# Low parts of P before the scores of the unit two ahead, on VectorE, in both attention stages

## The chip, the core and the metric

One core of a Trainium2 chip runs the whole program as one launch. The metric is the device time of that launch in microseconds. The program leaves PE (TensorE, matmuls and transposes), DVE (VectorE), ACT (ScalarE), POOL (GpSimd) and SP (the queue that issues most DMAs) to run their own instruction streams in order; they meet only at semaphores.

## The reference, cut to what matters

Two transformer blocks on a sequence of 1024 rows of width 1024. Each holds one attention stage.

```python
# first block: 6 query heads of 64, each block of 128 queries sees 3 blocks of keys
scores = jnp.einsum('bnqkgd,bnskd->bnkgqs', qb, kb).astype(jnp.float32) + bias
m = jnp.maximum(jnp.max(scores, axis=-1, keepdims=True), sink_l)
p = jnp.exp(scores - m)
p = p / (jnp.sum(p, axis=-1, keepdims=True) + jnp.exp(sink_l - m))
out = jnp.einsum('bnkgqs,bnskd->bnqkgd', p.astype(v.dtype), vb)
...
# second block: mixer A, 8 heads, windows of 128 keys behind the query, with a sink;
# mixer B, 8 heads, three dilated causal windows merged by their denominators
out_a = sink_swa_gqa(q_a, k_a, v_a, sinks[i], rel_bias[:, :A_Q_HEADS])
out_b = dilated_mixture(q_b, k_b, v_b, rel_bias[:, A_Q_HEADS:])
```

Around the attention stand the norms, the projections and the feed-forward layers, which the change leaves alone.

## The kernel before

The attention is cut into **units**: unit m is one block of 128 queries of one head, `b = m % 8`, so eight units make a head. A unit has as many blocks of 128 keys as the head's window asks for: two or three in the first stage (`att_bi`, 6 heads, 48 units), one or two in mixer A (the first 64 units of the second stage, `att_ab`), and b + 1, that is one to eight, in mixer B (the last 64 units, where the three dilated patterns are one causal mask with a table of biases). Four units make a **group**; a head has two.

The precise product is made of a high and a low part of each operand. So the softmax numerators P of a unit go through these steps:

- `scores(m)` on PE, L1823: two matmuls into one of two halves of PSUM (m % 2); it waits until the half was read by the scores of unit m-2.
- `score(m)` on DVE, L1946: adds the bias, writes `pr[m % 3]`, and its read-out `ast` of the row extreme counts `at_s`. It needs the scores in PSUM and the transposes of unit m-3 done.
- `exps(m)` on ACT, L1883: exp in place in `pr`, and a read-out of the row sums (`at_exp`).
- `turn_p(m)` on PE, L1833: transposes P into PSUM, in chunks of up to four blocks of keys. Units of up to four blocks have one chunk, larger ones two. Two PSUM banks take turns, so a chunk waits for the low part of the chunk two before it (`at_lo`).
- `high(m)` on ACT, L1893: the high part `ph` of each chunk (`at_hi`).
- `low_(m)` on DVE, L1956: the low part `pl`, PSUM minus `ph` (`at_lo`).
- After four units, `values(g)` on PE, L1848 (it waits for the last `low_` of the group), `denom(g)` on DVE, L1964 and L1966, `spread(g)` on PE, L1857, `spread_out(g)` on ACT, L1906, and `scale(g)` on DVE, L1975. For every second pair of groups ACT and POOL then split the result (L1911, L1999).

All orders are written out by hand. PE in loop m runs `scores(m + 2)`, `turn_p(m)`, and after the fourth unit one more `scores`, then `values` and `spread`. ACT in loop m runs `exps(m + 1)`, at a group's start `spread_out(g - 1)`, then `high(m)`:

```python
                if m + 1 < s.n:
                    exps(m + 1)
                if m % 4 == 0 and g:
                    spread_out(g - 1)
                high(m)
```

SP loads q and the bias table of head h once all scores of head h-2 are done on DVE (`at_s`, L1740, L1745); `scores` of a head's first unit waits for them.

Of the kernel before, what the change touches and what calls it, by code (L numbers as in the profile page):

```python
# [94 lines left out]
def build(nc, t, out, last=6):  # L95

    ctx = ExitStack()
    with ctx:
# [5 lines left out]
        def S(name):  # L104
            if name not in sems:
                sems[name] = ctx.enter_context(nc.semaphore(name))
            return sems[name]
# [1620 lines left out]
        def tab_dve(e):  # L1728
            e.wait_ge(S("oh_ld"), 48)
            e.memset(relb1[BUCKETS:BUCKETS + 1, :], 1.0).then_inc(S("rb"), 1)  # L1730
            e.tensor_copy(relb1[0:BUCKETS, :], relb[:]).then_inc(S("rb"), 1)
# [201 lines left out]
        def att_dve(e, s, a):  # L1933
            n, g_ = s.h0 * TT, s.h0 * 2
            e.wait_ge(S("sk_ld"), 32)

            def score(m):
                d, b, k0, k1, _ = s.units[m]
                w, r, j0 = (k1 - k0) * P, m % 8, (k0 - b) * P + d.off
                if m >= 3:  # L1940
                    e.wait_ge(S("at_tr"), s.unit_end(m - 3))
                if b == 0:
                    e.wait_ge(S(f"at_q_{s.name}{m // TT % 2}"), 48 * (m // TT // 2 + 1))
                e.wait_ge(S("at_qk"), n + m + 1)
                low = 3e30 if d.sink is None else nsk[:, d.sink:d.sink + 1]
                e.tensor_tensor_reduce(out=a.pr[m % 3][:, 0:w], in0=PSr[:, m % 2 * s.qs:m % 2 * s.qs + w],  # L1946
                                       in1=a.tab[m // TT % 2][:, j0:j0 + w], scale=-0.125, scalar=low, op0=ALU.add,
                                       op1=ALU.min, accum_out=ast[:, NM, r:r + 1]).then_inc(S("at_s"), 1)

            def low_(m):  # L1950
                _, b, _, _, chunks = s.units[m]
                _, kb0, _ = s.group(m // 4)
                for q, c0, c1 in chunks:
                    e.wait_ge(S("at_hi"), s.ch0 + q + 1)
                    o = (slice(None), slice(c0 - kb0, c1 - kb0), slice(b % 4 * P, (b % 4 + 1) * P))
                    e.tensor_tensor(a.pl[o], PS[:, 4 + q % 2, 0:(c1 - c0) * P].rearrange("p (k n) -> p k n", n=P),  # L1956
                                    a.ph[o].bitcast(F32), ALU.subtract).then_inc(S("at_lo"), 1)

            def denom(g):
                c = slice(4 * (g % 2), 4 * (g % 2) + 4)  # L1960
                e.wait_ge(S("at_exp"), n + 4 * g + 4)
                if s.units[4 * g][0].sink is not None:
                    e.wait_ge(S("at_es"), g_ + g + 1)
                    e.tensor_tensor(ast[:, DEN, c], ast[:, DEN, c], ast[:, ES, c], ALU.add).then_inc(S("at_dn"), 1)  # L1964
                    e.wait_ge(S("at_dn"), g_ + g + 1)
                e.reciprocal(ast[:, RD, c], ast[:, DEN, c]).then_inc(S("at_rd"), 1)  # L1966

            def scale(g):
                d = s.units[4 * g][0]
                e.wait_ge(S("at_pv"), g_ + g + 1)  # L1970
                e.wait_ge(S("at_rc"), g_ + g + 1)
                if g % 4 < 2 and g >= 8:
                    e.wait_ge(S("at_yl"), s.h0 + (g // 4 - 2) * 2 + g % 2 + 1)
                r = slice(d.row, d.row + HD)
                e.tensor_tensor(a.t[g // 4 % 2][d.half * HD:(d.half + 1) * HD, g % 2, :], PS[r, 6, :], a.rr[g % 2][r, :], ALU.mult)\  # L1975
                 .then_inc(S("at_nrm"), 1)

            score(0)
            score(1)
            if s is att_bi:  # L1980
                tab_dve(e)
            for m in range(s.n):
                if m + 2 < s.n:
                    score(m + 2)
                if m % 4 == 0 and m:
                    scale(m // 4 - 1)
                low_(m)
                if m % 4 == 3:
                    denom(m // 4)
            scale(s.n // 4 - 1)  # L1990
# [71 lines left out]
        with nc.Block() as block:  # L2062
# [85 lines left out]
            @block.vector  # L2148
            def _(e):
                prep_dve(e)  # L2150
                norm_out_dve(e, 0, 0)
                norm_out_dve(e, 0, 1)
                chain_dve(e)
                late_dve(e, 2)
                z_dve(e, 0)
                fft_dve(e)
                ssm_dve(e)
                att_dve(e, att_bi, mem_bi)
                out_dve(e, 0)
                for f, p in ((0, 1), (1, 2)):  # L2160
                    if last > p:
                        up_dve(e, f)
                        down_dve(e, p)
                if last > 3:
                    z_dve(e, 1)
                    att_dve(e, att_ab, mem_ab)
                    out_dve(e, 3)
                if last > 4:
                    up_dve(e, 2)
                    down_dve(e, 4)  # L2170
                if last > 5:
                    ple_dve(e)
# [53 lines left out]
```

## Time and profile before

| what | value |
|---|---|
| median of 3 runs | 3932.35 us (3929.28 to 3938.76) |
| the profiled execution | 3929.27 us, its span 3927.5 us |
| PE busy | 3391.6 us, 86% |
| DVE busy | 1193.1 us, 30% |
| ACT busy | 790.4 us, 20% |
| first attention stage | about 672 to 819 us of the span |
| second attention stage | about 2605 to 2919 us: mixer A to about 2717, mixer B after it |

The busy shares are those of the whole span. Outside the two stages PE is busy for nine tenths or more of most slices; within them no engine is, so the share of one engine tells little, and the order of steps and the waits between engines are what to read. A timeline row gives the start in us, the duration in us, engine, line, operation, tiles and, in brackets, how long the engine sat idle before and what released it.

### The profile page before, as it was taken

The numbers are of one execution on the slowest core, as the hardware profiler recorded it, in microseconds if no ns is written. First come the engines' busy times: TensorE is split into PE (matmuls) and PEld (weight loads), VectorE is DVE, ScalarE is ACT, GpSimd is POOL, SyncE is SP. The second block draws the span as 40 slices with busy tenths as digits, with TensorE's granted clock in tenths as the row PEclk, the third lists the DMA queues.
The fourth block names the chain that finished last, engine by engine and source line by source line (L and its number), as shares of the span: only waits on it lengthen the run. The fifth ranks groups of instructions, "written<-read, shape, count | busy, mean of one in ns | idle before, by whom it ended". The sixth has DMA issues, their size and how long they took to land.

```text
span 3927.5 us, 41626 instructions
## 1 busy us (share of the span) xinstructions
PE 3391.6 (86%) x15935; PEld 2811.4 (72%) x15935; DVE 1193.1 (30%) x1793; ACT 790.4 (20%) x1395; POOL 1553.2 (40%) x1271
## 2 busy tenths in 40 slices
PE   6773335589999999999999999987778999999977
PEld 4663324477888878888888888876667788888866
DVE  4754664425232322110001123135534100001323
ACT  3020003423111112110000122035533100001222
POOL 3137662044333346622323664210015223236743
PEclk8886666889999999999999999999999999999999
DMA  4551001552111124311112243444433111122432
GB/s 174 149 183 36 7 7 42 87 152 75 43 54 43 54 95 140 102 54 54 43 53 77 96 142 122 143 134 110 108 101 108 49 54 43 53 74 98 151 107 95
DMA packets 261327, 344.92 MB, mean 88 GB/s; under 512 B 24710, under 2 KB 203185, under 8 KB 261202
## 3 DMA queue, kind: packets, MB, share of 16 engines
q1 hardware_dynamic: 217784, 258.76, 21.8%
q10 hardware_dynamic: 43066, 84.01, 6.8%
q8 instruction: 84, 1.38, 0.1%
q0 software_dynamic: 352, 0.44, 0.0%
q14 instruction: 41, 0.34, 0.0%
HBM read 287.21 MB, written 55.95 MB: 87 GB/s over the span
## 4 chain that ended last, share of the span: by engine, by line
PE 75%; DVE 11%; ACT 5%; issue 3%; DMA 3%; POOL 2%; SPq 1%; ACTq 0%; DVEq 0%; POOLq 0%
PE PS L810 68%; PE PS L1848 3%; DMA tab_bi<-bias 1%; DVE ot L1591 1%; PE PS L746 1%; DVE pl_ab L1956 1%; DVE pt L679 1%; PE PS L1543 1%; DVE oo L1592 1%; ACT ph_ab L1893 1%; ACT act L701 1%; DVE t L1607 1%; PE PS L1833 1%; ACT pr_ab L1883 1%; ACT act L653 1%
## 5 line engine op out<-in xcount | busy, mean ns | idle before, releaser
L250 POOL TENSOR_TENSOR w_lo<-w_raw,w_hi 128x512 fp32r<-128x512 f32 x724 | 972.2, 1374 | 155.1 <-ACT w_hi L1302 130.4
L246 POOL CAST w_hi<-w_raw 128x2048 fp32r<-128x2048 f32 x173 | 335.6, 1940 | 1596.2 <-DMA w_raw<-ffn_w_gu 606.8
L810 PE MATMUL PS<-h_hi,w_hi 128*128 128x512 f32 x2482 | 803.2, 395 | 14.3 <-DVE h_lo L804 11.0
L810 PE MATMUL PS<-h_lo,w_hi 128*128 128x512 f32 x2482 | 795.7, 392 | 0.0
L810 PE MATMUL PS<-h_hi,w_lo 128*128 128x512 f32 x2482 | 795.7, 391 | 0.0
L810 PEld LDWEIGHTS PS<-h_hi,w_hi 128*128 128x128 f32 x2482 | 469.2, 189 | 114.6 <-DVE h_lo L804 15.6
L810 PEld LDWEIGHTS PS<-h_hi,w_lo 128*128 128x128 f32 x2482 | 469.2, 189 | 98.1
L810 PEld LDWEIGHTS PS<-h_lo,w_hi 128*128 128x128 f32 x2482 | 469.8, 189 | 95.2
L810 PE MATMUL PS<-w_hi,a_hi 128*128 128x512 f32 x1056 | 327.5, 392 | 11.0 <-DVE a_lo L876 7.2
L810 PE MATMUL PS<-w_lo,a_hi 128*128 128x512 f32 x1056 | 327.2, 391 | 0.0
L810 PE MATMUL PS<-w_hi,a_lo 128*128 128x512 f32 x1056 | 326.8, 391 | 0.0
L1044 DVE TENSOR_TENSOR aT<-act,PS 128x1024 f32 (+1 forms) x44 | 53.7, 1221 | 816.6 <-ACT act L1020 816.6
L876 DVE TENSOR_TENSOR a_lo<-aT,a_hi 128x1024 fp32r<-128x1024 f32 x66 | 92.5, 1401 | 537.3 <-ACT a_hi L873 537.3
L810 PEld LDWEIGHTS PS<-w_hi,a_hi 128*128 128x128 f32 x1056 | 199.1, 189 | 53.6 <-DVE a_lo L876 8.5
L810 PEld LDWEIGHTS PS<-w_hi,a_lo 128*128 128x128 f32 x1056 | 199.5, 189 | 41.6
L810 PEld LDWEIGHTS PS<-w_lo,a_hi 128*128 128x128 f32 x1056 | 199.3, 189 | 41.6
L810 PE MATMUL PS<-w_hi,h_hi 128*128 128x512 f32 (+2 forms) x640 | 193.8, 352 | 18.7 <-POOL h_lo L1999 7.0
L810 PE MATMUL PS<-w_hi,h_lo 128*128 128x512 f32 (+2 forms) x640 | 192.5, 350 | 0.0
L810 PE MATMUL PS<-w_lo,h_hi 128*128 128x512 f32 (+2 forms) x640 | 192.3, 350 | 0.0
L1020 ACT ACTIVATE act<-PS 128x1024 f32<-128x1024 f32 x44 | 45.2, 1026 | 716.7 <-PE PS L810 716.7
L873 ACT ACTIVATE a_hi<-aT 128x1024 fp32r (+1 forms) x66 | 69.7, 1060 | 560.4 <-PE PS L810 551.9
L810 PEld LDWEIGHTS PS<-w_hi,h_hi 128*128 128x128 f32 x640 | 122.6, 193 | 37.2 <-DVE pt L679 7.7
(281 smaller groups left out, 3630.3 us busy)
## 6 DMA issues: line engine op xcount, KB each, us to landing
w_raw<-ffn_w_gu SPq DMA_DIRECT2D x88, 512.0 KB, 4.6
w_raw<-ffn_w_down SPq DMA_DIRECT2D x88, 512.0 KB, 4.3
w_raw<-w_up SPq DMA_DIRECT2D x44, 512.0 KB, 5.0
w_raw<-w_down SPq DMA_DIRECT2D x44, 512.0 KB, 4.2
xs<-px ACTq DMA_DIRECT2D x40, 512.0 KB, 2.7
w_raw<-w_out SPq DMA_DIRECT2D x32, 512.0 KB, 4.5
w_raw<-w_in SPq DMA_DIRECT2D x28, 512.0 KB, 5.3
px<-xs ACTq DMA_DIRECT2D x7, 2048.0 KB, 10.4
```

Of the source, the lines that this page charges most:

```text
L246: e.tensor_copy(w_hi[b][:, 0:n], w_raw[b][:, 0:n]).then_inc(S("w_hi"), 1)
L250: op = e.tensor_tensor(w_lo[b][:, s], w_raw[b][:, s], w_hi[b][:, s].bitcast(F32), ALU.subtract)
L653: e.activation(act1[:], src, ACT.Square, accum_out=stat[:, 0, T:T + 1]).then_inc(S("n_sq"), 1)
L679: e.scalar_tensor_tensor(b.tmp[:], src, stat[:, 2, T:T + 1], b.g[:], ALU.mult, ALU.mult)\
L701: e.activation(act1[:], norm_row(n, T), ACT.Square, accum_out=stat[:, 3, T:T + 1]).then_inc(S("m_sq"), 1)
L746: mm = e.transpose(PS[:, norm_bank(q), i * P:(i + 1) * P], xrow(n, hf * 4 + i)[:, k * P:(k + 1) * P], ident[:])
L810: mm = e.matmul(o, a[ai], b[bi], start=start and first, stop=stop and end)
L873: e.activation(a_hi[b][:], src, ACT.Copy).then_inc(S("a_hi"), 1)
L876: e.tensor_tensor(a_lo[b][:], src, a_hi[b][:].bitcast(F32), ALU.subtract).then_inc(S("a_split"), 1)
L1020: e.activation(act1[:], gate, ACT.Silu).then_inc(S("f_act"), 1)
L1044: e.tensor_tensor(a, both(act1[:]), both(val), ALU.mult).then_inc(S("f_out"), 1)
L1848: mm = e.matmul(PS[:, 6, c], v[:, k, :], x[:, k - kb0, c], start=i == 0, stop=i == len(todo) - 1, skip_group_check=True)
```

## The change

In `att_dve` one line moves: in loop m the low parts of P of unit m are now made ahead of the scores of unit m+2 (and ahead of `scale`). Nothing else changes; PE, ACT, POOL and SP keep their instruction streams.

```diff
             for m in range(s.n):
+                low_(m)
                 if m + 2 < s.n:
                     score(m + 2)
                 if m % 4 == 0 and m:
                     scale(m // 4 - 1)
-                low_(m)
                 if m % 4 == 3:
                     denom(m // 4)
```

First place: VectorE in mixer A, from the scores of unit 5 of a head to the scores of the next head's unit 0 (tiles `pr_ab` and `tab_ab` are written and read by `score`, `pl_ab` by `low_`, `t_ab` by `scale`; the row `ast` behind a score is its read-out). Before:

```order
L1956 TENSOR_TENSOR pl_ab<-PS,ph_ab 128x2x128
L1964 TENSOR_TENSOR ast<-ast 128x4
L1966 RECIPROCAL ast<-ast 128x4
L1946 ISA pr_ab_220,ast<-PS,tab_ab_214,nsk 128x256
L1946 ISA ast 128x1
L1975 TENSOR_TENSOR t_ab_225<-PS,rr_ab_223 64x512
L1956 TENSOR_TENSOR pl_ab<-PS,ph_ab 128x2x128
L1946 ISA pr_ab_221,ast<-PS,tab_ab_214,nsk 128x256
L1946 ISA ast 128x1
```

With the change, the same stretch of VectorE:

```order
L1956 TENSOR_TENSOR pl_ab<-PS,ph_ab 128x2x128
L1946 ISA pr_ab_222,ast<-PS,tab_ab_214,nsk 128x256
L1946 ISA ast 128x1
L1964 TENSOR_TENSOR ast<-ast 128x4
L1966 RECIPROCAL ast<-ast 128x4
L1956 TENSOR_TENSOR pl_ab<-PS,ph_ab 128x2x128
L1946 ISA pr_ab_220,ast<-PS,tab_ab_214,nsk 128x256
L1946 ISA ast 128x1
L1975 TENSOR_TENSOR t_ab_225<-PS,rr_ab_223 64x512
```

The scores into `pr_ab_222` (unit 5) now stand behind the last low part of the old group, and those into `pr_ab_220` (unit 6) and `scale` behind the first low part of the new one.

Second place: VectorE in mixer B, the low parts of units 4 and 5 of a head, which have two chunks. Before:

```order
L1946 ISA pr_ab_221,ast<-PS,tab_ab_214 128x896
L1946 ISA ast 128x1
L1975 TENSOR_TENSOR t_ab_225<-PS,rr_ab_223 64x512
L1956 TENSOR_TENSOR pl_ab<-PS,ph_ab 128x4x128
L1956 TENSOR_TENSOR pl_ab<-PS,ph_ab 128x128
L1946 ISA pr_ab_222,ast<-PS,tab_ab_214 128x1024
```

With the change:

```order
L1956 TENSOR_TENSOR pl_ab<-PS,ph_ab 128x4x128
L1956 TENSOR_TENSOR pl_ab<-PS,ph_ab 128x128
L1946 ISA pr_ab_221,ast<-PS,tab_ab_214 128x896
L1946 ISA ast 128x1
L1975 TENSOR_TENSOR t_ab_225<-PS,rr_ab_223 64x512
L1956 TENSOR_TENSOR pl_ab<-PS,ph_ab 128x4x128
```

The scores of unit 6 (896 wide) stand behind both low parts of unit 4, those of unit 7 (1024 wide) behind both of unit 5.

## Rows read from the trace of the kernel before

**Rows 1.** Windows, mixer A and mixer B: busy us of each engine, PEclk, DMA share.

```profile
2610.00:2717.00 107.00, 76.25 (x506) 65.42 (x506) 60.86 (x231) 64.91 (x227) 8.43 (x7) 0.91 0.32 83
2717.00:2918.00 201.00, 154.25 (x849) 126.92 (x849) 105.34 (x259) 104.82 (x253) 10.85 (x10) 0.92 0.36 90
```

**Rows 2.** Timeline of DVE, mixer A, from one group's last low part to the next's.

```profile
2643.64 0.42 DVE L1956 TENSOR_TENSOR pl_ab<-PS,ph_ab 128x256 fp32r<-128x256 f32 x1
...
2647.54 0.40 DVE L1956 TENSOR_TENSOR pl_ab<-PS,ph_ab 128x256 fp32r<-128x256 f32 x1
...
2649.28 0.42 DVE L1956 TENSOR_TENSOR pl_ab<-PS,ph_ab 128x256 fp32r<-128x256 f32 x1 [0.33 <-ACT ph_ab L1893]
2649.62 0.47 DVE L1946 CUSTOM_DVE_ANT_0 pr_ab<-PS,tab_ab,nsk 128x256 f32<-128x256 f32 x1
...
2650.02 0.42 DVE L1956 TENSOR_TENSOR pl_ab<-PS,ph_ab 128x256 fp32r<-128x256 f32 x1
```

**Rows 3.** Timeline of ACT in the same stretch.

```profile
2646.72 0.38 ACT L1893 ACTIVATE ph_ab<-PS 128x256 fp32r<-128x256 f32 x1
2646.98 0.51 ACT L1883 ACTIVATE pr_ab<-pr_ab,ast 128x256 f32<-128x256 f32 x1
...
2647.47 0.38 ACT L1893 ACTIVATE ph_ab<-PS 128x256 fp32r<-128x256 f32 x1
...
2650.14 0.51 ACT L1883 ACTIVATE pr_ab<-pr_ab,ast 128x256 f32<-128x256 f32 x1
```

**Rows 4.** Timeline of DVE in one head of mixer B.

```profile
2772.28 0.29 DVE L1956 TENSOR_TENSOR pl_ab<-PS,ph_ab 128x128 fp32r<-128x128 f32 x1
...
2776.38 0.17 DVE L1966 RECIPROCAL ast<-ast 128x4 f32<-128x4 f32 x1
...
2780.43 0.87 DVE L1956 TENSOR_TENSOR pl_ab<-PS,ph_ab 128x512 fp32r<-128x512 f32 x2
2781.22 1.21 DVE L1946 CUSTOM_DVE_ANT_0 pr_ab<-PS,tab_ab 128x1024 f32<-128x1024 f32 x1
...
2788.36 0.17 DVE L1966 RECIPROCAL ast<-ast 128x4 f32<-128x4 f32 x1
```

**Rows 5.** Timeline of ACT in that head.

```profile
2771.34 0.27 ACT L1893 ACTIVATE ph_ab<-PS 128x128 fp32r<-128x128 f32 x1
...
2782.66 1.15 ACT L1883 ACTIVATE pr_ab<-pr_ab,ast 128x1024 f32<-128x1024 f32 x1
```

**Rows 6.** Timeline of the first stage, one group after a landed load.

```profile
751.93 0.38 ACT L1893 ACTIVATE ph_bi<-PS 128x256 fp32r<-128x256 f32 x1
...
752.74 0.41 DVE L1956 TENSOR_TENSOR pl_bi<-PS,ph_bi 128x256 fp32r<-128x256 f32 x1
...
755.84 0.56 DVE L1956 TENSOR_TENSOR pl_bi<-PS,ph_bi 128x384 fp32r<-128x384 f32 x1
```

**Rows 7.** Timeline of SP and PE, the load of head 3, first stage.

```profile
716.04 0.44 SPq L1740 DMA_DIRECT2D q_bi<-qkh  x1
...
745.12 0.58 PE L1823 MATMUL PS<-k2h_bi,q_bi 128*128 128x256 f32 x1 [14.95 <-DMA tab_bi<-bias]
```

**Rows 8.** Waits of the first stage: us in total, times, longest.

```profile
PEld PS L1823 <- DMA tab_bi<-bias: 31.5, 2, 16.3
```

**Rows 9.** Windows between two values: in mixer A, and in mixer B.

```profile
2646.00:2650.40 4.40, 2.53 (x18) 1.87 (x16) 3.14 (x12) 3.60 (x13) 0.00 (x0) 1.00 0.14 33
...
2803.90:2813.30 9.40, 5.12 (x37) 4.02 (x34) 6.69 (x16) 7.61 (x18) 1.28 (x1) 1.00 0.50 117
```

**Rows 10.** Timeline of PE, first eight matmuls of values, two heads of mixer B.

```profile
2813.40 3.14 PE L1848 MATMUL PS<-ph_ab,vvh_ab 128*128 128x512 f32 x8 [1.22 <-DVE pl_ab L1956]
...
2837.54 1.76 PE L1848 MATMUL PS<-ph_ab,vvh_ab 128*128 128x512 f32 x8 [1.22 <-DVE pl_ab L1956]
```

**Rows 11.** Timeline of ACT, waiting for spread after 15 matmuls of values, twice.

```profile
2652.93 0.60 ACT L1906 ACTIVATE rr_ab<-PS 128x512 f32<-128x512 f32 x1 [2.19 <-PE PS L1857]
...
2667.95 0.60 ACT L1906 ACTIVATE rr_ab<-PS 128x512 f32<-128x512 f32 x1 [4.13 <-PE PS L1857]
```

## The prediction

> **What bounds the kernel now.** The page first: outside the two attention stages PE is full, and the change touches nothing there. So I read windows of the stages. In mixer A and mixer B the three engines that share a unit's work are all short of full: PE 76.25 of 107 us, DVE 60.86, ACT 64.91 in A, and 154, 105 and 105 of 201 in B [rows 1]. No engine is the bound; a chain through all of them is. I then followed it in the timeline of one group of mixer A. From the last low part of a group to the first of the next takes 3.90 us, and the next three low parts come within 2.48 us, 0.83 us apiece [rows 2]. The 3.90 us is values, spread and the copy on ACT: dense work on PE and no gain to be had. In the 2.48 us DVE and ACT run side by side: while ACT makes exp and high part of one unit, DVE already has the scores of the unit after it behind it. That lead is what the change moves.
>
> **The new chain.** ACT's order is fixed: exp of unit m+2 stands ahead of the high part of m+1. Before, the scores of m+2 did not need the low part of m. Now they are queued behind it. So each unit must pass: low part of m, scores of m+2, exp of m+2, high part of m+1, low part of m+1. It is a closed loop between two engines, and no step of it can overlap another. PE's transposes of m+1 need only the exp of m+1 and an older low part, so they are ready and hide under it. Behind the waiting low part DVE now holds the scores and `scale`; who waits for them is ACT's exp, and behind that exp the high parts.
>
> **Mixer A.** For two blocks of keys: a low part holds DVE for 0.34 us (2649.28 to 2649.62), the scores with their read-out 0.40 and 0.08, and 0.04 to the exp (2649.62 to 2650.14, 0.52 in all) [rows 2, 3]; exp to the high part behind it 0.49 (2646.98 to 2647.47), high part 0.38 and 0.02 to the next engine, 0.40 [rows 3]. Sum 1.75 us. The last link of a head's second group has the next head's one-block unit in it, some 0.12 and 0.11 less (slopes below), 1.52. Three links are 1.75 + 1.75 + 1.52 = 5.02 us instead of 2.48.
>
> The edge of the group gains: the first high part ended at 2647.10 and its low part began at 2647.54, behind `scale` [rows 2, 3]. Now it goes first: 3.49 instead of 3.90 us. New group 8.5 us against 6.38, so +2.1, and 16 groups give **+34 us**. `scale` costs nothing in its new place: 0.61 us of DVE under an exp and a high part of 0.87. `denom` behind one more scores is hidden as well: 1.2 us after the low part, while values run for some 1.5.
>
> **Mixer B.** Units have 1 to 8 blocks. Scores to exp: 0.52 at two blocks, 1.21 + 0.04 at eight, so 0.12 a block [rows 2, 4]; exp to high part 0.49 and 1.15, 0.11 a block [rows 3, 5]; high part of the first chunk 0.27 at one block, 0.38 at two, so 0.60 at four [rows 3, 5]; low part 0.34 at two, 0.79 for four plus one (2780.43 to 2781.22), 0.13 a block [rows 2, 4]. A link to unit k takes scores and exp of k+1, the first high chunk and all low parts of k. By these lines the links to units 1, 2 and 3 take 1.98, 2.45 and 2.92 us, 7.35 together; before, from 2772.49 (0.21 behind the start of the low part) to 2776.38, 3.89 [rows 4]. The links to 5, 6 and 7 take 3.72, 4.09 and 2.60, 10.41; before, 2781.22 to 2788.36, 7.14 [rows 4]. Gained: the low part of unit 0 waited from 2771.61 to 2772.28, 0.64 [rows 4, 5]. So a head pays 3.46 + 3.27 - 0.64 = 6.1 us, eight heads **+49 us**.
>
> **First stage.** Three blocks: links of 0.64 + 0.60 + 0.51 + 0.47 = 2.22 us, 6.66 for three against 3.10 before; edge -0.40 (high part ends at 752.31, low part began at 752.74) [rows 6]: +3.2 a group. The other group of a head has two-block units, +2.5 by the same lines; mean 2.8. But a part is hidden by loads. The load of head 3 is issued at 716.04, when the scores of head 1 are done, and PE stands until 745.12, of which 15 us idle [rows 7]; there are two such waits, 31.5 us [rows 8]. Head 2's eight units run under that load, and so do head 4's under the next: 6 us more fit in 15. What counts is the way to the scores of unit 15 (3.5 groups), from the landing to the scores of unit 31 (1.5) and the last two groups: 7 x 2.8 = **+20 us**, if the load takes its 29 us again. Were nothing hidden, 12 groups would be 34.
>
> Sum of the loops: 34 + 49 + 20 = 103 us.
>
> **The clock.** PE's share between two values falls. In A it is 2.53 of 4.40 us (57%) at granted clock 1.00, in B 5.12 of 9.40 (54%) [rows 9]; the same work over 2.1 to 3.3 us more is about 40% in both. And at the end of such a B stretch the first eight matmuls of values took 3.14 us in one head and 1.76 in another [rows 10]: the lower of the two levels (1.2 GHz) and the upper (2.4). Six of the eight heads show the low one there. In A it was one group in the middle of the stage, where ACT waited 4.13 us for spread instead of 2.19 [rows 11]: 1.94 us a time. At 40% I take the frequency of B's denser stretches, six in eight, for every group: 14 groups of A, 8 first groups of B, which were at the upper level, and 7 exposed ones of the first stage, 29 x 0.75 x 1.9 = **+41 us**. Bounds: 0, and with all 29 and B's two remaining second groups (1.4 each) 58. What PE does inside the loop is not on its path, so a slower transpose costs nothing more.
>
> A rule of the Trainium skill speaks to this: the page TensorE: Matmul & The Clock Gate, section Part 4: PE-mode transpose, says that transposes do not count as busy time for the clock in the way matmuls do. No row here separates the two; by it the stretches, which are half transposes, would be lower still, and the sum would be the third case below.
>
> Total 103 + 41 = 144 us on the profiled execution of 3929.27 us (span 3927.5), 4073; the median of the runs is 3 us above that execution, so 4076 us.
>
> **The rivals.**
> - Forecast: loop closed, clock low at most values. 4076; its own range 4045 to 4100. Chance 0.50.
> - Loop closed, clock stays up: PE's gaps inside a loop are only 1 to 1.5 us long. 3932 + 103 = 4035. For it, the same load in one B head stayed up [rows 10]; against it, six heads. 0.20.
> - Clock low at every values: 3932 + 103 + 58 = 4093, up to 4105 if the stretch on the lower level outlasts values. 0.18.
> - The loop is half open: the longer links overlap more than the single rows say, or the loads of the first stage take over more. 3932 + 52 = 3984. Every link is a semaphore or a queue order, so little for it. 0.08.
> - Not slower: the early low part decides. It saves 0.4 us at 44 group edges, 18 us, so 3914, if a link costs no more than it did, that is if a link of the loop fits in 0.83 us. It would need exp of m+2 not to stand ahead of the high part of m+1; the four steps of the link are 1.75 us. Below 0.1 us more a link it would decide. 0.04.
>
> **How the numbers follow.** The range reaches from the second case less some 12 us for what was at the low level before and for the loads, to the third case plus 18 us for the interpolated links (a tenth of 103, and 8 for the loads): 4020 to 4112; the last two cases and half a tenth at each end lie outside. Faster by over 0.3% (12 us, about what can be told from no change) 0.025, the same 0.015, slower 0.96.
>
> **What would show it.** Mixer A: groups 8.5 us apart, on DVE the low part, then the scores, then idle for 0.9 us behind a high part; ACT idle before nearly each exp, released by DVE's `ast`. Mixer A about 141 to 165 us long instead of 107, B 250 to 265 instead of 201. Low part of the first unit right behind its high part, `scale` behind it. The two waits for the bias table shorter by 5 to 6 us each, the loads again 29 us. The granted clock in both stages near 0.7, and eight matmuls of values at 3.1 us in most groups. The out, up and down stages unchanged to a microsecond. I would be wrong if the scores of m+2 ran while the high part of m was still being made, if ACT had exps to run during the loop, or if the clock stayed at 1.00.

## The result, and the profile after

| what | before | after |
|---|---|---|
| median of 4 runs each | 3935.34 us (3929.28 to 3938.76) | 4082.24 us (4075.38 to 4085.41) |
| the profiled execution | 3929.27 us, span 3927.5 | 4079.91 us, span 4078.1 |
| mean granted TensorE clock | 0.932 | 0.909 |

The ratio is 1.0373, 95% interval 1.0352 to 1.0394: slower by 3.7%. The forecast was 4076 us, in a range of 4020 to 4112.

The page first. The busy time of DVE and ACT hardly moved (1193.1 to 1192.6 us and 790.4 to 801.3), PE shows 102 us more:

```profile
span 4078.1 us, 41626 instructions
PE 3493.8 (86%) x15935; PEld 2880.7 (71%) x15935; DVE 1192.6 (29%) x1793; ACT 801.3 (20%) x1395; POOL 1551.7 (38%) x1271
```

So 150.6 us of span were added by an edit that gives VectorE no more to do. PE's busy time is longer with the same instructions; the granted clock in the windows below is lower. Windows of mixer A and of mixer B (mixer B's with its end), which answer to [rows 1]; columns as there:

```profile
2660.00:2817.00 157.00, 110.65 (x510) 89.63 (x511) 61.78 (x229) 66.67 (x219) 8.90 (x7) 0.73 0.24 60
2817.00:3070.00 253.00, 175.55 (x832) 138.82 (x830) 106.26 (x253) 107.66 (x246) 11.46 (x9) 0.82 0.26 66
```

Mixer A has the same 62 and 67 us of DVE and ACT in 157 us instead of 107, at a mean clock of 0.73 instead of 0.91.

The edges of windows cut a stage in different places, so for the balance I cut the span at events of the trace: the first `score` of the first stage, its last ACT copy `rr_bi` (L1906), and the copies `rr_ab` number 0, 16 and 31 of the second stage. Number 0 to 16 stands for mixer A and 16 to 31 for mixer B. A copy comes behind the values of its group, so the row of mixer A takes in the links of mixer B's first group, and the row of mixer B has the links of 15 groups, not 16.

| us | before | after | difference | predicted |
|---|---|---|---|---|
| ahead of the first stage | 673.0 | 677.7 | +4.7 | 0 |
| first stage | 143.1 | 177.5 | +34.4 | 20 + 10 clock |
| between the stages | 1803.9 | 1808.5 | +4.6 | 0 |
| mixer A | 109.0 | 167.0 | +58.0 | 34 + 20 clock |
| mixer B | 186.7 | 235.8 | +49.1 | 49 + 11 clock |
| behind it | 1011.7 | 1011.6 | -0.1 | 0 |

The clock column splits the predicted 41 us by its 7, 14 and 8 group edges. The pieces outside the stages carry no reading: the first of them is the same program in all kernels of this document and lay between 672.5 and 681.4 us in thirteen of their executions, and at 696.3 in one. So 9 of the 150.6 us lie where nothing was changed, and the three stages account for 141.5.

**The link of mixer A.** Timeline of DVE and ACT for one link of the changed kernel, from the low part of one unit to that of the next:

```profile
2738.14 0.42 DVE L1956 TENSOR_TENSOR pl_ab<-PS,ph_ab 128x256 fp32r<-128x256 f32 x1 [0.22 <-ACT ph_ab L1893]
2738.48 0.47 DVE L1946 CUSTOM_DVE_ANT_0 pr_ab<-PS,tab_ab,nsk 128x256 f32<-128x256 f32 x1
2739.00 0.51 ACT L1883 ACTIVATE pr_ab<-pr_ab,ast 128x256 f32<-128x256 f32 x1 [0.37 <-DVE ast L1946]
2739.50 0.36 ACT L1893 ACTIVATE ph_ab<-PS 128x256 fp32r<-128x256 f32 x1
2739.90 0.42 DVE L1956 TENSOR_TENSOR pl_ab<-PS,ph_ab 128x256 fp32r<-128x256 f32 x1 [0.94 <-ACT ph_ab L1893]
```

This is the loop as forecast: low part, scores, exp, high part, low part, one after the other. The brackets say that each engine waited for the other: ACT's exp for DVE's `ast`, DVE's low part for ACT's `ph_ab`, 0.94 us. The link is 2739.90 - 2738.14 = 1.76 us against a forecast of 1.75, and 0.83 before [rows 2]. The view of waits over the whole second stage says how often (us in total, times, longest):

```profile
DVE pl_ab L1956 <- ACT ph_ab L1893: 239.3, 136, 7.7
ACT pr_ab L1883 <- DVE ast L1946: 128.6, 126, 2.0
```

Of 128 exps 126 waited for the scores. Counted over the row of mixer A in the balance, DVE and ACT were busy at the same time for 20 of 167 us, against 52 of 109 before.

**The values at either level.** Timeline of PE, the first matmuls of values in two groups of mixer A and in one head of mixer B:

```profile
2742.14 1.11 PE L1848 MATMUL PS<-ph_ab,vvh_ab 128*128 128x256 f32 x4 [0.85 <-DVE pl_ab L1956]
2752.17 1.33 PE L1848 MATMUL PS<-ph_ab,vvh_ab 128*128 128x128 f32 x5 [0.46 <-DVE pl_ab L1956]
...
2874.84 3.14 PE L1848 MATMUL PS<-ph_ab,vvh_ab 128*128 128x512 f32 x8 [0.77 <-DVE pl_ab L1956]
2890.32 0.85 PE L1848 MATMUL PS<-ph_ab,vvh_ab 128*128 128x512 f32 x4 [1.08 <-DVE pl_ab L1956]
```

The four matmuls of 256 columns take 1.11 us where four at the upper level take 0.68 (a row of an experiment below), the five of a head's other group 1.33 where they took 0.79 before: all 16 groups of mixer A show the lower level (1.2 GHz). In mixer B the eight of a head's second group answer to [rows 10], and all eight heads begin them at the lower level (3.14 us), but the four of the first group take 0.85 to 0.87 in seven heads of eight, which is the upper level (2.4 GHz).

### The profile page after: what moved, and what is told of

It is laid out like the page before. It is cut to its first block, busy times and chain, and to the rows that moved or that the text cites. A ratio compares the mean times of both kernels' runs of the same rounds, so it can differ in the third digit from the quotient of the medians.

```text
span 4078.1 us, 41626 instructions
## 1 busy us (share of the span) xinstructions
PE 3493.8 (86%) x15935; PEld 2880.7 (71%) x15935; DVE 1192.6 (29%) x1793; ACT 801.3 (20%) x1395; POOL 1551.7 (38%) x1271
## 4 chain that ended last, share of the span: by engine, by line
PE 74%; DVE 11%; ACT 6%; issue 3%; DMA 3%; POOL 2%; SPq 1%; ACTq 0%; DVEq 0%; POOLq 0%
PE PS L810 65%; PE PS L1848 4%; ACT pr_ab L1883 1%; DVE pr_ab L1946 1%; DMA tab_bi<-bias 1%; DVE ot L1591 1%; ACT ph_ab L1893 1%; PE PS L746 1%; DVE pl_ab L1956 1%; DVE pt L679 1%; PE PS L1543 1%; DVE oo L1592 1%; PE PS L1531 1%; ACT act L701 1%; PE PS L1857 1%
## 5 line engine op out<-in xcount | busy, mean ns | idle before, releaser
L810 PEld LDWEIGHTS PS<-h_hi,w_hi 128*128 128x128 f32 x2482 | 468.7, 189 | 116.0 <-DVE h_lo L804 16.5
L1999 POOL TENSOR_TENSOR h_lo<-t_ab,h_hi 128x512 fp32r<-128x512 f32 x16 | 20.4, 1272 | 415.3 <-ACT h_hi L1911 415.3
```

Source lines behind the costliest of these rows:

```text
L810: mm = e.matmul(o, a[ai], b[bi], start=start and first, stop=stop and end)
```

## The experiments

Twelve more kernels ran. Lengths of mixer A and B and of the first stage are cut as in the balance above. They had one execution each, but for the last comparison. Seventeen executions of the kernel before lay between 3925.66 and 3950.63 us, so stages are compared rather than totals. Stages scatter too where their order is the same: the first stage and mixer B of the kernel before took 140.7 to 146.0 us and 182.3 to 186.7 in five kernels each, and mixer A 109.0 to 115.4 in three.

**One stage at a time.** The low part goes ahead of the scores in one of the three stages only, by a condition in `att_dve`:

```diff
             for m in range(s.n):
+                first = s is att_bi      # only_a: s is att_ab and m < 64; only_b: s is att_ab and m >= 64
+                if first:
+                    low_(m)
                 if m + 2 < s.n:
                     score(m + 2)
                 if m % 4 == 0 and m:
                     scale(m // 4 - 1)
-                low_(m)
+                if not first:
+                    low_(m)
```

> The low part goes first only in the first attention stage. In the changed kernel that stage and the wait before the output projection took 34 us more (start of the projection 39.1 us later, of which 4.7 us were there before the stage began). If each stage pays by itself: about 34 us longer in that stage, nothing in the second, whole 3967. If the second stage's loss needed the first one's (a lower clock carried over), the two would not add up.

> Low part first only in mixer A (the first 64 units of the second stage). Closed loop plus low clock: values to values 10.25 us a group instead of 6.55, mixer A about 56 us longer, mixer B as before, whole 3990. If the loop were only partly the cause, B would change as well, since the units after the last of A start from another state.

> Low part first only in mixer B. Closed loop: 6.1 to 6.5 us a head, B about 50 us longer, A as before, whole 3985. Read with it: the short values (first group of a head) at the upper clock as in the changed kernel, so that no clock term is paid in B.

| us | total (the kernel before, run beside them: 3929.2) | first stage | mixer A | mixer B |
|---|---|---|---|---|
| before | 3929.27 | 143.1 | 109.0 | 186.7 |
| only first stage | 3965.86 | **178.1** | 112.6 | 182.3 |
| only mixer A | 3991.85 | 146.0 | **164.8** | 182.6 |
| only mixer B | 3989.55 | 140.8 | 115.4 | **238.5** |

Each stage pays for itself: +35.0, +55.8 and +51.8 us where the order was changed, and within 7 us of before where it was not. The three add up to 142.6 us, against 141.5 for the three stages in the full change; the differences of the totals, 36.7 + 62.7 + 60.4 = 159.8 us, carry the scatter of four executions. So no stage's price depends on another's by more than the scatter.

**Where the loop closes.** The loop needs two orders: DVE's, with the low part first, and ACT's, with the exp of m+1 ahead of the high part of m. So ACT's was opened, on the changed kernel and on the one before:

```diff
-                if m + 1 < s.n:
-                    exps(m + 1)
                 if m % 4 == 0 and g:
                     spread_out(g - 1)
                 high(m)
+                if m + 1 < s.n:
+                    exps(m + 1)
```

> The changed kernel, and on ScalarE the high part of unit m ahead of the exp of unit m+1. That opens the loop at the other engine: the low part no longer waits for an exp that waits for scores that wait for the last low part. It closes another one on ScalarE and TensorE: exp of m+1, transposes of m+1, high part of m+1, about 0.6 + 0.4 + 0.4 = 1.45 us in mixer A instead of 1.76. Theory of the loop: a link in A 1.4 to 1.5 us, whole 4030 to 4060. Rival (scores behind the low part cost by their own place on VectorE, whatever ScalarE does): a link stays at 1.76 and the whole at 4080 or more.

> The kernel before with ScalarE's order alone changed (high part of m ahead of the exp of m+1). Beside the same change made to the changed kernel (stages 170.9, mixer A 162.4, mixer B 215.2 us) it tells whether the low part's place costs anything once the loop through ScalarE's exp is open. Theory of the loop: ScalarE's own loop sets both, so the three stretches within 3% of those three, with low parts first even a little ahead. Rival (the place on VectorE costs by itself): this one clearly shorter, mixer A below 140 and B near 193.

Changed kernel with ACT opened: 4054.09 us, mixer A 161.4, mixer B 209.1, first stage 167.4. The one before with it: 4030.46 us (3938.43 without, beside it), mixer A 162.4, mixer B 210.5, first stage 161.2. (The expectation's 162.4, 215.2 and 170.9 us for the first of the two are not cut as in the balance.) The place of the low part had cost 58.0 and 49.1 us in the mixers and 34.4 in the first stage; with ACT's order opened it costs -1.0, -1.4 and +6.2. So the loop of the prediction needs the pair of orders. It isn't a cure, though: the new order of ACT has a loop of its own, as its timeline of the changed kernel shows:

```profile
2750.63 0.38 ACT L1893 ACTIVATE ph_ab<-PS 128x256 fp32r<-128x256 f32 x1 [0.78 <-PE PS L1833]
2750.91 0.50 ACT L1883 ACTIVATE pr_ab<-pr_ab,ast 128x256 f32<-128x256 f32 x1
...
2752.28 0.38 ACT L1893 ACTIVATE ph_ab<-PS 128x256 fp32r<-128x256 f32 x1 [0.78 <-PE PS L1833]
```

Now the exp waits for nothing and the high part waits 0.78 us for PE's transposes: high part, exp of the next unit, its transposes, its high part, 2752.28 - 2750.63 = 1.65 us. The expectation had this loop at 1.4 to 1.5. It takes 1.39 between the high parts at 2720.43 and 2721.82, in a stretch with a granted clock of 0.90, and 1.65 here, at 0.50: PE's transposes lie on this loop (two of them take 0.44 us there and 0.69 here), so a link pays for the clock, which a link of 1.76 in the changed kernel does not. This loop, not DVE, sets the pace in both of these kernels, and makes the one before 92 us slower. It also limits what the pair shows: the loop through DVE no longer sets the pace, but a smaller cost of the low part's place would be hidden under 1.65 us a link.

**Work on VectorE, on the loop and off it.** 45 fills of a part of `pr` that no mixer A unit reads, 0.30 us of DVE each from the fill's start to that of the scores or low part behind it (0.39 where `scale` follows), put in three places:

```diff
                 low_(m)
+                if s is att_ab and m < 60 and m % 4 != 3:      # dve_on
+                    e.memset(a.pr[m % 3][:, 512:896], 0.0)
                 if m + 2 < s.n:
                     score(m + 2)
+                # dve_off: the same two lines here; dve_before: here too, in the kernel before
```

> The changed kernel with one extra memset (128x384, some 0.2 to 0.45 us, into columns of pr that mixer A does not use) on VectorE between the low part and the scores, for three units in four of mixer A. In a closed loop every such piece lies on the path: 45 of them make mixer A longer by 45 times its duration, some 10 to 20 us. If VectorE had slack there, nothing.

> The changed kernel with the same 45 memsets of mixer A, now on VectorE behind the scores instead of ahead of them. Behind the scores VectorE idles some 0.9 us until the next high part, so in a closed loop they cost nothing: mixer A 167 us as without them, against 182.6 with them ahead of the scores. If VectorE's work in all were what counts, 180 or more again.

> The kernel before with the same 45 memsets behind the scores. There VectorE is nearly full between two values (0.3 us idle in 2.5), so most of their 0.29 us apiece shows: mixer A 109 + 8 to 13 = 117 to 122 us, more than in the changed order, where they are free.

| us | total | mixer A | against its parent |
|---|---|---|---|
| between low part and scores, changed kernel | 4095.65 | 182.6 | +15.6 |
| behind the scores, changed kernel | 4083.43 | 171.0 | +4.0 |
| behind the scores, kernel before | 3939.42 | 120.0 | +11.0 |

On the loop the fills cost all of their 45 x 0.29 = 13.1 us, as a link grew from 1.76 to 2.05, and the group edges a little more. Behind the scores in the changed kernel they cost a quarter of the 15.6, where the expectation had nothing. DVE's timeline there shows why, and where the rest comes from:

```profile
2743.50 0.42 DVE L1956 TENSOR_TENSOR pl_ab<-PS,ph_ab 128x256 fp32r<-128x256 f32 x1 [4.00 <-ACT ph_ab L1893]
...
2744.36 0.38 DVE L1987 MEMSET pr_ab<- 128x384 f32 x1
2744.75 0.69 DVE L1975 TENSOR_TENSOR t_ab<-PS,rr_ab 64x512 f32<-64x512 f32 x1
2745.47 0.42 DVE L1956 TENSOR_TENSOR pl_ab<-PS,ph_ab 128x256 fp32r<-128x256 f32 x1
...
2746.32 0.38 DVE L1987 MEMSET pr_ab<- 128x384 f32 x1
2747.23 0.42 DVE L1956 TENSOR_TENSOR pl_ab<-PS,ph_ab 128x256 fp32r<-128x256 f32 x1 [0.53 <-ACT ph_ab L1893]
```

In an ordinary link the fill lies in DVE's wait, which shrinks from 0.94 to 0.53 us, and the link stays 1.76. At a group's start `scale` already fills that wait; fill and `scale` together make it 1.97, some 0.2 us in each of 15 groups. In the kernel before, the same fills cost 11.0 us: an ordinary group grew by 0.3 to 0.4 us (from copy to copy 6.39 to 6.76, 6.82 to 7.11), 5 us in all, so DVE was close to the path there too, and the rest went where more groups stood at the lower clock (9.05 us instead of 6.8). "DVE has slack at 30% busy" would have been a wrong reading of either kernel.

**The clock.** To separate the loop from the clock, PE was given matmuls that nobody waits for (identity times identity into an unused part of PSUM), behind the transposes of mixer A's first 60 units: nine in a group of four units, on both kernels, and then eleven, on the changed one.

```diff
                 turn_p(m)
+                if s is att_ab and m < 60 and m % 4 != 3:
+                    for _ in range(3):
+                        e.matmul(PSr[:, 512:640], ident[:], ident[:], start=True, stop=True)
+                # fill_all: every m < 60, with range(3 if m % 4 != 3 else 2)
```

> The changed kernel with three extra matmuls of the identity by itself behind the transposes of three units in four, mixer A alone, into columns of PSUM that nobody reads: work for TensorE in its idle time, to hold its clock up. Clock term: if the clock then stays at 1.00, a group falls from 10.25 to about 8.7 us and mixer A from 166 to 140 to 145. If the loop's links were slow for another reason than the clock at the edges, it stays at 160 or more.

> The same extra matmuls in the kernel before, as a control. There 14 of 16 groups have the upper clock already; the extra matmuls can only save the two low ones, 3 us, and may delay transposes. Mixer A 107 to 115 us against 110.

> The changed kernel with extra matmuls behind the transposes of every unit of mixer A's first 60 (three, and two for the fourth of a group, where values follow). With three units in four they brought mixer A from 167.0 to 159.2 us, and the clock fell during values. If the gap ahead of values was what let it fall, it now stays at the upper level and mixer A takes 140 to 147 us. If not, 155 to 160 again.

| us | total | mixer A | granted clock, 2670 to 2820 us |
|---|---|---|---|
| changed | 4079.91 | 167.0 | 0.74 |
| with nine | 4081.7 | 159.2 | 0.83 |
| with eleven | 4064.89 | 145.1 | 0.94 |
| before, with nine | 3939.21 | 108.9 (109.0 without) | |

Windows of that stretch for the last of the changed kernels and for the changed kernel itself:

```profile
2670.00:2820.00 150.00, 122.74 (x836) 104.18 (x834) 69.68 (x239) 74.75 (x232) 10.18 (x8) 0.94 0.29 72
```

```profile
2670.00:2820.00 150.00, 105.50 (x491) 85.43 (x491) 59.37 (x219) 64.05 (x210) 8.90 (x7) 0.74 0.27 65
```

With eleven the clock is up at the start of every values of the first 15 groups, and mixer A is 21.9 us shorter **with more work on PE**. What is left, 145.1 - 109.0 = +36 us, is the loop, but for a group or two that stand at the lower level on either side (one in the kernel before, the last two here). Its timeline of DVE and PE, with the edge of a group:

```profile
2746.88 0.42 DVE L1959 TENSOR_TENSOR pl_ab<-PS,ph_ab 128x256 fp32r<-128x256 f32 x1 [0.94 <-ACT ph_ab L1896]
...
2747.36 0.68 PE L1848 MATMUL PS<-ph_ab,vvh_ab 128*128 128x256 f32 x4 [0.86 <-DVE pl_ab L1959]
...
2750.38 0.42 DVE L1959 TENSOR_TENSOR pl_ab<-PS,ph_ab 128x256 fp32r<-128x256 f32 x1 [2.39 <-ACT ph_ab L1896]
```

The edge is 2750.38 - 2746.88 = 3.50 us at the upper level (the same edge in the changed kernel, 2721.18 to 2726.16, is 4.98), and the three links behind it end at 2755.43, 5.05 us later. The links are as long at the upper level as at the lower. Nine matmuls were not enough, and the expectation of 140 to 145 us was missed: some groups stayed up and others fell, one of them while values were running:

```profile
2707.03 0.97 PE L1848 MATMUL PS<-ph_ab,vvh_ab 128*128 128x128 f32 x5 [0.75 <-DVE pl_ab L1959]
2707.80 1.27 PE L1848 MATMUL PS<-pl_ab,vvh_ab 128*128 128x128 f32 x5
2708.87 1.27 PE L1848 MATMUL PS<-ph_ab,vvl_ab 128*128 128x128 f32 x5
```

That kernel's total did not fall either: its mixer B took 244.1 us instead of 235.8, with the first values of three heads at the lower level instead of one. In the kernel before, the nine matmuls brought all 16 values of mixer A to the upper level, which saved 2 us in one group, and cost the others some 0.1 us each, so nothing was gained.

**The early low part alone.** The rival "not slower" counted 0.4 us saved at each of 44 group edges, if only the links cost nothing. The edges' part of the change was built by itself: scores stay first, only `scale` and the low part change places.

```diff
                 if m + 2 < s.n:
                     score(m + 2)
+                low_(m)
                 if m % 4 == 0 and m:
                     scale(m // 4 - 1)
-                low_(m)
```

> The kernel before, in which only scale and the low part behind it change places (the scores of unit m+2 stay ahead of both). It keeps the gain at a group's edge (first low part 0.4 to 0.6 us earlier) without closing the loop. By the gain counted for the edges, 44 x 0.4 = 18 us faster. But VectorE is nearly full until the next values, and scale then lies ahead of the next scores and low part: I expect within 0.3%, at most 8 us faster.

It is slower by 0.3%, where at most 8 us faster was expected: 3943.59 us median of 12 against 3932.6 of 17, ratio 1.0031, interval 1.0014 to 1.0049. Timeline from the ACT copy of `spread` (L1906) on, in this kernel:

```profile
2666.66 0.60 ACT L1906 ACTIVATE rr_ab<-PS 128x512 f32<-128x512 f32 x1 [1.90 <-PE PS L1857]
...
2667.57 0.42 DVE L1956 TENSOR_TENSOR pl_ab<-PS,ph_ab 128x256 fp32r<-128x256 f32 x1 [2.21 <-ACT ph_ab L1893]
...
2668.02 0.68 DVE L1975 TENSOR_TENSOR t_ab<-PS,rr_ab 64x512 f32<-64x512 f32 x1
2668.74 0.48 DVE L1946 CUSTOM_DVE_ANT_0 pr_ab<-PS,tab_ab,nsk 128x256 f32<-128x256 f32 x1
```

and in the kernel before, an edge that differs only in ACT's split (L1911), which the first has and this one has not:

```profile
2674.35 0.60 ACT L1906 ACTIVATE rr_ab<-PS 128x512 f32<-128x512 f32 x1 [1.89 <-PE PS L1857]
...
2675.03 0.69 DVE L1975 TENSOR_TENSOR t_ab<-PS,rr_ab 64x512 f32<-64x512 f32 x1 [2.13 <-issue]
...
2675.76 0.42 DVE L1956 TENSOR_TENSOR pl_ab<-PS,ph_ab 128x256 fp32r<-128x256 f32 x1
2676.10 0.47 DVE L1946 CUSTOM_DVE_ANT_0 pr_ab<-PS,tab_ab,nsk 128x256 f32<-128x256 f32 x1
```

Counted from the copy, the low part begins at 0.91 instead of 1.41 us: the 0.5 us gain is real. But the scores behind it begin at 2.08 instead of 1.75, because DVE stands idle from 0.68 to 0.91 with `scale` ready behind it. ACT's exp waits for those scores: at edges without the split it sat idle 0.85 us until they were done in this kernel (exp at 2689.98) and 0.61 in the kernel before (2683.31). In the old order `scale` filled a hole; the low part that I called late was not what the next link waited for. At the upper clock a group of mixer A takes 6.61 or 7.17 us from copy to copy instead of 6.39 or 6.83, so the edge costs 0.2 to 0.3 us where the rival had it save 0.4. In this execution mixer A is 116.8 us long (+7.8), mixer B 188.0 (+1.3), the first stage 147.0 (+3.9); part of the 7.8 is four groups of 8.0 to 9.1 us at a lower clock, where the kernel before has one.

## Why the prediction was right, point by point

**The new chain** held in every part. Measured against forecast in mixer A: link 1.76 (1.75), three links 5.04 to 5.15 (5.02), edge at the upper clock 3.50 (3.49; the other kind of edge, into a head's first group, 3.72), `scale` and `denom` hidden. DVE's part of the loop is shown by the fills: between low part and scores they cost their full length, behind the scores nothing in an ordinary link. The order of ACT as the other half is shown by the pair with ACT opened, as far as that pair goes. The rivals "half-open loop", "not slower" and "clock stays up" are out.

**Mixer A** was forecast at +34 for the loop and +20 for the clock. The eleven extra matmuls separate the two: +36 and 21.9. The sum, +58.0, is 4 us over the forecast's 54.

**Mixer B** was forecast at +49 for the links and +11 for the clock, 60 in all; measured were +49.1. DVE in one head of the changed kernel, from the end of a low part (the row behind it):

```profile
2882.71 0.29 DVE L1956 TENSOR_TENSOR pl_ab<-PS,ph_ab 128x128 fp32r<-128x128 f32 x1 [7.50 <-ACT ph_ab L1893]
2882.92 0.55 DVE L1946 CUSTOM_DVE_ANT_0 pr_ab<-PS,tab_ab 128x384 f32<-128x384 f32 x1
...
2889.58 0.69 DVE L1956 TENSOR_TENSOR pl_ab<-PS,ph_ab 128x512 fp32r<-128x512 f32 x1 [1.47 <-ACT ph_ab L1893]
2890.19 0.95 DVE L1946 CUSTOM_DVE_ANT_0 pr_ab<-PS,tab_ab 128x768 f32<-128x768 f32 x1
...
2894.07 0.89 DVE L1956 TENSOR_TENSOR pl_ab<-PS,ph_ab 128x512 fp32r<-128x512 f32 x2 [2.84 <-ACT ph_ab L1893]
2894.88 1.08 DVE L1946 CUSTOM_DVE_ANT_0 pr_ab<-PS,tab_ab 128x896 f32<-128x896 f32 x1
...
2902.67 0.28 DVE L1946 CUSTOM_DVE_ANT_0 pr_ab<-PS,tab_ab 128x128 f32<-128x128 f32 x1
...
2905.05 0.69 DVE L1956 TENSOR_TENSOR pl_ab<-PS,ph_ab 128x512 fp32r<-128x512 f32 x1 [0.16 <-ACT ph_ab L1893]
2905.65 0.41 DVE L1946 CUSTOM_DVE_ANT_0 pr_ab<-PS,tab_ab 128x256 f32<-128x256 f32 x1
```

The first three links take 2890.19 - 2882.92 = 7.27 us (forecast 7.35), the last three 2905.65 - 2894.88 = 10.77 (10.41). The second miss lies in the last link, 2905.65 - 2902.67 = 2.98 us against 2.60. Unit 7's two low parts take 1.46 of it instead of 1.20, as the second had to wait for its own high part (0.16 us), which the forecast left out.

From copy to copy, like can be compared with like. The stretch with a head's first group took 8.13 to 8.29 us before and 11.02 to 11.04 after, with its values at the upper level in both: +2.8, as forecast (3.46 - 0.64). The stretch with its second group took 14.4 us before in the two heads whose values stood at the upper level and 15.9 to 17.7, mean 16.8, in the six at the lower one; after it took 19.7 to 20.2, mean 19.8, all at the lower: +3.1 against a forecast of 3.27. Over the 7 and 8 stretches of this row that makes 44 us for the loop (46 by the forecast's terms; its 49 had the eighth first group too). The other 5 us are the two heads that fell to the lower level, 2.4 us each (the forecast's bound counted 1.4, from the first eight matmuls alone). So the term of the clock was too large by half, and on the wrong groups: the first groups, which I thought would fall, stayed at the upper level in seven heads of eight. This split is worked out from rows and no run shows it apart, as none filled PE in mixer B.

How near 49.1 comes to 49 is luck, and it depends on the execution. Before, the values of two to five heads stood at the upper level, and the five kernels with the old order in mixer B took 182.3 to 186.7 us, mean 183.7, in that row; the one that the balance uses was the longest. The six with the new order took 235.8 to 244.1, mean 239.0. By the means mixer B pays 55 us.

**First stage:** +34.4 against 20 + 10. The link is 1.15 us of idle DVE and 2.24 us long (forecast 2.22). By its pieces: from the first scores to the load of head 3, 58.4 us instead of 43.0, +15.4, where 3.5 groups of 2.8 us and 3.5 edges at the clock's 0.75 x 1.9 made 14.8. The load took its 29 us again (736.07 to 765.54):

```profile
736.07 0.44 SPq L1740 DMA_DIRECT2D q_bi<-qkh  x1
...
765.54 0.58 PE L1823 MATMUL PS<-k2h_bi,q_bi 128*128 128x256 f32 x1 [6.36 <-DMA tab_bi<-bias]
...
791.53 0.44 SPq L1740 DMA_DIRECT2D q_bi<-qkh  x1
792.66 0.39 PE L1823 MATMUL PS<-k2h_bi,q_bi 128*128 128x256 f32 x1 [4.51 <-DMA tab_bi<-bias]
```

From the landing to the issue of head 5's load it took 26.0 us instead of 16.5, +9.5, where 1.5 groups gave 6.3: this is the term that was too small. Two group edges lie in it, not one and a half, and both were at the lower clock (five matmuls of values 1.65 and 1.54 us instead of 0.97 and 0.93), as all twelve of the stage were, and the stretch ends in a whole link of a new group. The last piece gave +9.1 against 8.4. A third wait for the table, head 4's 4.51 us, was not foreseen either; it hid behind head 5's load, whose wait sets the time after it. The table's waits are 18.3 us in three instead of 31.5 in two [rows 8].

**The clock** as a whole: 41 us forecast. Measured 21.9 in mixer A, worked out as 5 in mixer B, and in the first stage all group edges at the lower level where I took three in four. The size was right in A by luck: every group was low there, not three in four, but each cost about 1.5 us (edges of 4.98 instead of 3.50), not 1.9. The case "clock low at every values" was thus true of mixer A and the first stage and false of half of mixer B.

**The total** came nearer than its parts. Mixer A and the first stage cost 4 us each more than forecast, mixer B 11 less, which leaves 3 us less than the forecast 144 in the stages; the 9 us of scatter outside them make the 150.6.

The page TensorE: Matmul & The Clock Gate of the Trainium skill, section Part 4: PE-mode transpose, says that transposes do not count for the clock as matmuls do. The traces can't tell. In the changed kernel mixer A's stretches between values, about half scores and half transposes, all led to the lower level. In the kernel before, the same matmuls and transposes in less time (in the first stretch of [rows 9] PE has scores running for 1.86 us and transposes for 1.61, with some overlap) led to the upper one at 14 of 16. No run here swapped transposes for matmuls of the same length, and the eleven extra matmuls added load as well as changing its kind. Whether transposes count differently here stays open.

## What to carry to other kernels

When two in-order engines work on a pipeline of units, write down for every step which unit it serves and follow the orders and semaphores once around: if moving one step makes a path from unit m to unit m+1 through both engines, the time of a unit becomes the sum of that path, however idle the engines are. A step that starts "late" is a gain only if the next thing on the path waits for it; ask also what stood in the hole it leaves (here `scale` had been filling it). And when a change makes the matmul engine wait more, price its clock as a term of its own: here it was nearly four tenths of the loss in mixer A. And measure the piece that is to be explained in more than one execution before a term is said to fit: mixer B alone moved by 4 us between executions that are the same there before, and by 8 after.

## What the runs showed of the hardware that was not expected

- The granted clock settled into the pattern of the work: low at all 16 values of mixer A, and in mixer B low at the longer and high at the shorter values of seven heads of eight. With the new order in mixer B the second groups began their values at the lower level in all eight heads of six kernels; with the old one in three to six heads of eight, in five kernels.
- The clock fell inside a dense run of 15 matmuls (0.97, then 1.27 us for five) when the stretch ahead of it had been filled with nine extra matmuls, and with eleven it stayed up. Extra work on PE made mixer A 21.9 us shorter.
- Dense work does not guarantee the upper level. In the changed kernel with ACT opened, the early projection from 202 us on ran for 41.2 us instead of 21.8, with PE busy all the time, at a granted clock of 0.50. Its group of matmuls in the profile of that kernel, and in the one before (busy us, mean ns):

```profile
L810 PE MATMUL PS<-w_hi,h_hi 128*128 128x128 f32 x64 | 26.6, 416 | 0.0
```

```profile
L810 PE MATMUL PS<-w_hi,h_hi 128*128 128x128 f32 x64 | 17.8, 278 | 0.0
```

  That lies ahead of the attention and has nothing to do with the change; it is why that kernel's total, 4054.09, is not read against its twin's. What set it off is open.
